# Prompt attention on one core: an extra full-array matmul into an unread bank at each of TensorE's two waits per unit

## The chip, the cores and the metric

The kernel runs on one core of a Trainium2 chip. The metric is the device time of one launch in microseconds (us). Three runs of the kernel before gave 5847.97, 5851.65 and 5852.48 us; their median is 5851.65 us.

## What is computed

The reference is one inference step of a trunk of two layers, for a prompt of 512 tokens and for 8 requests of 8 new tokens each. A layer projects the normalised rows, passes them through three mixers (pooling, dilated attention, a recurrent mixer), maps them back, and adds a block of retrieved experts. The change lies in the dilated attention of the prompt alone: 6 heads of width 64, where each query reads keys at three strides.

```python
def dilated_attn_prompt(q, k, v):
    scale = HEAD_DIM ** -0.5
    for window, dil in DILATED_GROUPS:            # (128, 1), (512, 4), (2048, 16)
        ...
        s = jnp.einsum('brnqhd,brnkhd->brnhqk', qr, kb, preferred_element_type=jnp.float32) * scale
        s = jnp.where(valid[None, None, :, None], s, NEG_INF)
        m = jnp.max(s, axis=-1, keepdims=True)
        p = jnp.exp(s - m)
        den = jnp.sum(p, axis=-1, keepdims=True)
        o = jnp.einsum('brnhqk,brnkhd->brnqhd', p / den, vb.astype(jnp.float32))
        ...
    return _combine_branches(outs, lses).astype(q.dtype)
```

The kernel joins the three branches into one softmax over all 512 keys: how often a query reads a key enters as the logarithm of that count, added to the scores (0 times is a large negative number).

## The kernel before

`program` (from L2199) loops over the two layers. In each, `attend_prompt` (L475) comes after `rotate` and before `attend_sample`; it is a stage of its own, with all engines starting it together and ending it together.

Its work is cut into 24 units, `units = [(qt, h) ...]`: four query tiles `qt` of 128 queries, and in each the six heads `h`. A unit of query tile `qt` reads `qt + 1` tiles of 128 keys, so units grow from one key tile (the first six) to four (the last six). For one unit:

- TensorE makes the scores, `scores(u)` at L505: the head's 64 rows of q against 128, 256, 384 or 512 keys, into one of three banks of `s_ps`. Only 64 of the array's 128 rows are in use.
- VectorE scales them and adds the logarithm of the counts (L559), and takes the maximum (L562). ScalarE takes the exponential with its sum (L535). VectorE inverts the sum (L577) and scales the row (L578), which gives semaphore `normed`.
- TensorE transposes the probabilities, 128 keys at a time, against the identity (L516) into `t_ps`; ScalarE copies them out (L545, semaphore `turned_in`).
- TensorE multiplies them with the values (L524): 64 columns of v, 128 rows, into `o_ps`. VectorE copies the result into `mixed` (L569).

All data are float32. In the trace a matmul of two float32 operands is two records, each with its own weight load; a transpose is one record.

TensorE's order is written out by hand. It first issues the scores of units 0, 1 and 2. Then, for each unit `u`: wait for `normed` of this unit; transposes of `u`; scores of `u + 3` (none for the last three units); wait for `turned_in` of this unit; values of `u`. VectorE and ScalarE run ahead of it: the probabilities and the transposed probabilities have two buffers each, the scores three banks.

`s_ps` takes three of the eight banks of the accumulation memory, `t_ps` and `o_ps` two each; one is free. Before unit 0 can be transposed, the counts `att_lc` have to arrive by DMA; they are issued at the stage's start. `m.ident` is the 128 by 128 identity, `m.proj` holds the projected rows (pooling input, q, k, v), 576 columns each.

Of the kernel before, what the change touches and what calls it, by code (L numbers as in the profile page):

```python
# [29 lines left out]
F32 = mybir.dt.float32  # L30
# [7 lines left out]
P = 128  # L38
# [55 lines left out]
def sbuf(nc, name, shape, dt):  # L94
    return nc.sbuf_tensor(f"{name}_{next(_serial)}", shape, dt)


def psum(nc, name, shape, dt):
    return nc.psum_tensor(f"{name}_{next(_serial)}", shape, dt)
# [15 lines left out]
@contextmanager  # L115
def stage(nc, *names):

    with ExitStack() as ctx:
        sems = namedtuple("Semaphores", names)(*(ctx.enter_context(nc.semaphore(f"{n}_{next(_serial)}")) for n in names))
        with nc.Block() as block:  # L120
            yield block, sems
        with nc.Block() as tidy:  # L122
            @tidy.sync
            def _(sp):
                for sem in sems:
                    sp.sem_clear(sem)
# [348 lines left out]
def attend_prompt(nc, m):  # L475


    units = [(qt, h) for qt in range(4) for h in range(HEADS)]
    with ExitStack() as ctx:
        sm = ctx.enter_context(sbuf(nc, "att_s", [P, 2, TP_], F32))  # L480
        pr = ctx.enter_context(sbuf(nc, "att_p", [P, 2, TP_], F32))
        pt = ctx.enter_context(sbuf(nc, "att_pt", [P, 2, 4, P], F32))
        st_ = ctx.enter_context(sbuf(nc, "att_stat", [P, 2, 4], F32))
        lc = ctx.enter_context(sbuf(nc, "att_lc", [P, 4, TP_], F32))
        s_ps = ctx.enter_context(psum(nc, "att_sps", [P, 3, TP_], F32))
        t_ps = ctx.enter_context(psum(nc, "att_tps", [P, 2, 4, P], F32))
        o_ps = ctx.enter_context(psum(nc, "att_ops", [P, 2, 512], F32))
        with stage(nc, "counts_in", "scored", "maxed", "expd", "normed", "turned", "turned_in", "valued",
                   "out_in", "dve_step", "stored") as (block, s):
            @block.sync  # L490
            def _(sp):
                sp.dma_start(lc[:], m.dram.count_prompt).then_inc(s.counts_in, 16)
                sp.dma_start(m.dram.out_k[m.l], m.proj[:, BK:BK + PAIRS, :]).then_inc(s.stored, 16)
                sp.dma_start(m.dram.out_v[m.l], m.proj[:, BV:BV + PAIRS, :]).then_inc(s.stored, 16)
                sp.wait_ge(s.stored, 32)

            @block.tensor
            def _(pe):
                def scores(u):
                    qt, h = units[u]  # L500
                    c, o = h // 2, 64 * (h % 2)
                    n = (qt + 1) * P
                    if u >= 3:
                        pe.wait_ge(s.maxed, u - 2)
                    nc.tensor.matmul(s_ps[:, u % 3, 0:n], m.proj[o:o + 64, BQ + c, qt * P:(qt + 1) * P],  # L505
                                     m.proj[o:o + 64, BK + c, 0:n], start=True, stop=True).then_inc(s.scored, 1)

                for u in range(3):
                    scores(u)
                for u, (qt, h) in enumerate(units):  # L510
                    c, o = h // 2, 64 * (h % 2)
                    pe.wait_ge(s.normed, u + 1)
                    if u >= 2:
                        pe.wait_ge(s.turned_in, u - 1)
                    for b in range(qt + 1):
                        ins = nc.tensor.transpose(t_ps[:, u % 2, b, :], pr[:, u % 2, b * P:(b + 1) * P], m.ident[:])  # L516
                    ins.then_inc(s.turned, 1)
                    if u + 3 < len(units):
                        scores(u + 3)
                    pe.wait_ge(s.turned_in, u + 1)  # L520
                    if u >= 2:
                        pe.wait_ge(s.out_in, u - 1)
                    for b in range(qt + 1):
                        ins = nc.tensor.matmul(o_ps[o:o + 64, u % 2, 0:P], m.v_tok[:, b, h * HD:(h + 1) * HD],  # L524
                                               pt[:, u % 2, b, :], start=(b == 0), stop=(b == qt))
                    ins.then_inc(s.valued, 1)

            @block.scalar
            def _(act):
                def exps(u):  # L530
                    n = (units[u][0] + 1) * P
                    act.wait_ge(s.maxed, u + 1)
                    if u >= 2:
                        act.wait_ge(s.turned, u - 1)
                    nc.scalar.activation(pr[:, u % 2, 0:n], sm[:, u % 2, 0:n], ACT.Exp, bias=st_[:, u % 2, 0:1],  # L535
                                         accum_out=st_[:, u % 2, 1:2]).then_inc(s.expd, 1)

                exps(0)
                for u, (qt, h) in enumerate(units):
                    if u + 1 < len(units):  # L540
                        exps(u + 1)
                    act.wait_ge(s.turned, u + 1)
                    if u >= 2:
                        act.wait_ge(s.valued, u - 1)
                    nc.scalar.activation(pt[:, u % 2, 0:qt + 1, :], t_ps[:, u % 2, 0:qt + 1, :],  # L545
                                         ACT.Copy).then_inc(s.turned_in, 1)

            @block.vector
            def _(dve):
                st = Steps(dve, s.dve_step)  # L550
                dve.wait_ge(s.counts_in, 16)

                def mask_max(u):
                    qt = units[u][0]
                    n = (qt + 1) * P
                    dve.wait_ge(s.scored, u + 1)
                    if u >= 2:
                        dve.wait_ge(s.expd, u - 1)
                    st.link(nc.vector.scalar_tensor_tensor(out=sm[:, u % 2, 0:n], in0=s_ps[:, u % 3, 0:n],  # L559
                                                           scalar=HD ** -0.5, in1=lc[:, qt, 0:n],  # L560
                                                           op0=ALU.mult, op1=ALU.add))
                    nc.vector.tensor_reduce(st_[:, u % 2, 0:1], sm[:, u % 2, 0:n], X, ALU.max,  # L562
                                            negate=True).then_inc(s.maxed, 1)

                def collect(u):
                    qt, h = units[u]
                    c, o = h // 2, 64 * (h % 2)
                    dve.wait_ge(s.valued, u + 1)
                    nc.vector.tensor_copy(m.mixed[o:o + 64, 2 + c, qt * P:(qt + 1) * P],  # L569
                                          o_ps[o:o + 64, u % 2, 0:P]).then_inc(s.out_in, 1)  # L570

                mask_max(0)
                mask_max(1)
                for u, (qt, h) in enumerate(units):
                    n = (qt + 1) * P
                    dve.wait_ge(s.expd, u + 1)
                    st.link(nc.vector.reciprocal(st_[:, u % 2, 2:3], st_[:, u % 2, 1:2]))  # L577
                    nc.vector.tensor_scalar(pr[:, u % 2, 0:n], pr[:, u % 2, 0:n], st_[:, u % 2, 2:3], None,  # L578
                                            ALU.mult).then_inc(s.normed, 1)
                    if u + 2 < len(units):  # L580
                        mask_max(u + 2)
                    if u >= 1:
                        collect(u - 1)
                collect(len(units) - 1)
# [1827 lines left out]
```

## Time and profile before

| | us |
|---|---|
| median of three runs | 5851.65 |
| the profiled execution, device time | 5854.53 |
| its span, from first to last instruction | 5852.7 |
| TensorE matmul busy | 5207.9 (89% of the span) |
| TensorE weight load busy | 4825.6 (82%) |
| VectorE busy | 3272.7 (56%) |
| ScalarE busy | 1733.5 (30%) |
| GpSimd busy | 353.5 (6%) |

The profile comes from one execution; positions are counted from its first instruction. Most of the span is the experts' block, where TensorE is busy over 90%. The stage that is changed stands at about 223 to 307 us in the first layer and 3140 to 3221 us in the second, so some 160 us of the whole.

The profile lists the clock that the chip granted TensorE in each stretch, as a share of 2.4 GHz: 1.00 is 2.4 GHz and 0.50 is 1.2 GHz, and there is no third level on this core. The mean over the span is 0.914. A group of matmuls is listed with its start, its extent and its count; a matmul's extent reaches past the start of the next one, since matmuls are pipelined, so what one of them costs is read from the distance between starts.

### The profile page before, as it was taken

To read this page: it belongs to the slowest core of one execution; us is meant where nothing else is said; L and a number is where in the kernel's file an instruction comes from. 1 tells how busy PE (TensorE), PEld (TensorE's weight loads), DVE (VectorE), ACT (ScalarE), POOL (GpSimd) and SP (SyncE) were. 2 spreads that over 40 slices of the span, in tenths; PEclk is the share of its full clock that TensorE was granted. 3 is DMA by queue.
4 is the path that set the end of the run, shared out by engine and by line. 5 is a ranking of instruction groups with operands and counts; after the bars stand their busy time and mean duration, and the time that the engine had idled before them with its cause. 6 is when DMAs were issued, how large, how long until landed. Compare 5 with 4: busy or idle time off the path is not lost. (4 is left out here: it accounts for less than half of the span.)

```text
span 5852.7 us, 96170 instructions
## 1 busy us (share of the span) xinstructions
PE 5207.9 (89%) x36954; PEld 4825.6 (82%) x36954; DVE 3272.7 (56%) x7049; ACT 1733.5 (30%) x2854; POOL 353.5 (6%) x192
## 2 busy tenths in 40 slices
PE   6887877888999999999978878678889999999998
PEld 6636747888999999999966367478889999999998
DVE  2436456777555555556724354577875555555567
ACT  2213213278222222222122132122872222222222
POOL 0010004400000000000000100045000000000000
PEclk9787768999999999999987877789999999999999
DMA  2150002256433323334321500121564332333253
GB/s 84 44 188 3 0 36 84 68 148 198 172 117 126 126 112 119 126 119 162 126 73 38 190 0 0 49 78 64 171 196 158 126 119 112 126 126 118 106 180 127
DMA packets 387666, 631.22 MB, mean 108 GB/s; under 512 B 25952, under 2 KB 324448, under 8 KB 345632
## 3 DMA queue, kind: packets, MB, share of 16 engines
q1 hardware_dynamic: 387488, 628.99, 30.8%
q8 instruction: 94, 1.54, 0.1%
q14 instruction: 84, 0.69, 0.0%
HBM read 526.51 MB, written 152.36 MB: 116 GB/s over the span
## 5 line engine op out<-in xcount | busy, mean ns | idle before, releaser
L235 PE MATMUL ex_op<-ex_ah,ex_vl 128*128 128x288 f32 x3584 | 1064.2, 297 | 7.4 <-DVE ex_acc L2081 6.4
L237 PE MATMUL ex_op<-ex_ah,ex_vh 128*128 128x288 f32 x3584 | 1059.5, 296 | 0.0
L236 PE MATMUL ex_op<-ex_al,ex_vh 128*128 128x288 f32 x3584 | 1058.7, 295 | 0.0
L2081 DVE TENSOR_TENSOR ex_acc<-ex_acc,ex_op 128x576 f32<-128x576 f32 x896 | 672.7, 754 | 551.4 <-PE ex_op L237 544.3
L235 PE MATMUL ex_hp<-x_hi,ex_ul 128*128 128x288 f32 x3072 | 907.0, 295 | 37.9 <-PEq L122 37.9
L237 PE MATMUL ex_hp<-x_hi,ex_uh 128*128 128x288 f32 x3072 | 907.7, 295 | 0.0
L236 PE MATMUL ex_hp<-x_lo,ex_uh 128*128 128x288 f32 x3072 | 906.8, 295 | 0.0
L235 PEld LDWEIGHTS ex_op<-ex_ah,ex_vl 128*128 128x128 f32 x3584 | 674.9, 188 | 14.9 <-DVE ex_acc L2081 14.9
L237 PEld LDWEIGHTS ex_op<-ex_ah,ex_vh 128*128 128x128 f32 x3584 | 675.0, 188 | 0.0
L236 PEld LDWEIGHTS ex_op<-ex_al,ex_vh 128*128 128x128 f32 x3584 | 674.9, 188 | 0.0
L235 PEld LDWEIGHTS ex_hp<-x_hi,ex_ul 128*128 128x128 f32 x3072 | 578.6, 188 | 38.3 <-issue 38.3
L2030 ACT ACTIVATE ex_vh<-ex_v 128x2048 fp32r<-128x2048 f32 x128 | 245.5, 1918 | 1141.9 <-PE ex_op L237 862.4
L236 PEld LDWEIGHTS ex_hp<-x_lo,ex_uh 128*128 128x128 f32 x3072 | 578.6, 188 | 0.0
L237 PEld LDWEIGHTS ex_hp<-x_hi,ex_uh 128*128 128x128 f32 x3072 | 578.5, 188 | 0.0
L2084 DVE TENSOR_TENSOR ex_a<-ex_a,ex_g 128x576 f32<-128x576 f32 x192 | 145.6, 758 | 634.2 <-ACT ex_a L2044 633.7
L2044 ACT ACTIVATE ex_a<-ex_hp 128x576 f32<-128x576 f32 x192 | 124.9, 651 | 799.1 <-PE ex_hp L237 799.1
L1789 PE MATMUL g_ps<-g_a,g_a 128*128 128x128 f32 x2304 | 314.1, 280 | 46.9 <-DVE g_a L1752 22.8
L1789 PEld LDWEIGHTS g_ps<-g_a,g_a 128*128 128x128 f32 x2304 | 289.8, 194 | 58.2 <-DVE g_a L1752 38.8
L2073 DVE TENSOR_TENSOR ex_vl<-ex_v,ex_vh 128x2048 fp32r<-128x2048 f32 x128 | 292.5, 2285 | 0.0
L235 PE MATMUL rt_qps<-x_hi,rt_wl 128*128 128x288 f32 x512 | 161.4, 315 | 100.3 <-ACT rt_q L1607 84.9
L235 PE MATMUL proj_ps<-x_hi,proj_w_lo 128*128 128x288 f32 x704 | 211.7, 301 | 41.3 <-DVE proj_w_lo L317 41.3
L1752 DVE TENSOR_SCALAR g_a<-iota,i1T,gT 128x128 f32<-128x128 f32 x864 | 248.3, 350 | 0.0
(366 smaller groups left out, 9939.6 us busy)
## 6 DMA issues: line engine op xcount, KB each, us to landing
ex_u<-in_peer_uT SPq DMA_DIRECT2D x128, 1024.0 KB, 7.6
ex_v<-in_peer_v SPq DMA_DIRECT2D x128, 1024.0 KB, 6.8
gate_matrix<-g_stage SPq DMA_DIRECT2D x18, 4096.0 KB, 15.9
ex_g<-gate_matrix SPq DMA_DIRECT2D x128, 576.0 KB, 5.0
dec_k<-in_cache_kT SPq DMA_DIRECT2D x16, 1536.0 KB, 7.1
dec_v<-in_cache_v SPq DMA_DIRECT2D x16, 1536.0 KB, 7.5
out_s_k<-in_cache_k_kept SPq DMA_DIRECT2D x128, 190.5 KB, 6.2
out_s_v<-in_cache_v_kept SPq DMA_DIRECT2D x128, 190.5 KB, 6.2
```

What stands on the lines that cost most here:

```text
L235: nc.tensor.matmul(out, w_lo, x_hi, start=first, stop=False)
L236: nc.tensor.matmul(out, w_hi, x_lo, start=False, stop=False)
L237: return nc.tensor.matmul(out, w_hi, x_hi, start=False, stop=last)
L1752: ins = nc.vector.tensor_scalar(a1[:, b % 4, n, :], m.iota[:], i1T[:, t], gT[:, t], ALU.is_equal, ALU.mult)
L1789: ins = nc.tensor.matmul(ps[:, q, n, :], a2[:, q, n, :], a1[:, q, n, :], start=True, stop=True)
L2030: nc.scalar.activation(v_hi[:, j], v_raw[:, j], ACT.Copy).then_inc(s.vh, 1)
L2044: nc.scalar.activation(a_raw[:, e, :].rearrange("p (a t) -> p a t", a=2), hp[:, e, :, 0:HALF], ACT.Gelu).then_inc(s.gelud, 1)
L2073: nc.vector.tensor_tensor(v_lo[:, j], v_raw[:, j], v_hi[:, j].bitcast(F32), ALU.subtract).then_inc(s.vl, 1)
L2081: nc.vector.tensor_tensor(a, a, o[:, :, 0:HALF], ALU.add).then_inc(s.added, 1)
L2084: nc.vector.tensor_tensor(a_raw[:, e, :].rearrange("p (u t) -> p u t", u=NU), h.rearrange("p (u t) -> p u t", u=NU), gb[:, j, :, e, :], AL ...
```

## The change

TensorE gets a bank of its own, `warm`, that nobody reads, and a helper `keep_busy` that issues one float32 matmul into it: the identity as weights (128 by 128), 256 columns of `m.proj` as the moving operand. The helper is called twice per unit: ahead of the wait for `normed`, and ahead of the wait for `turned_in`. Nothing else moves, and no wait is added or removed.

```diff
@@ -485,6 +485,7 @@
         o_ps = ctx.enter_context(psum(nc, "att_ops", [P, 2, 512], F32))
+        warm = ctx.enter_context(psum(nc, "att_warm", [P, 512], F32))
@@ -507,8 +508,13 @@
                 for u in range(3):
                     scores(u)
+                def keep_busy():
+
+                    nc.tensor.matmul(warm[:, 0:256], m.ident[:], m.proj[:, 0, 0:256], start=True, stop=True)
+
                 for u, (qt, h) in enumerate(units):
                     c, o = h // 2, 64 * (h % 2)
+                    keep_busy()
                     pe.wait_ge(s.normed, u + 1)
@@ -517,6 +523,7 @@
                     if u + 3 < len(units):
                         scores(u + 3)
+                    keep_busy()
                     pe.wait_ge(s.turned_in, u + 1)
```

Over two layers of 24 units that is 96 matmuls, 192 records of matmul and 192 weight loads.

## Rows read from the trace of the kernel before

**Rows 1.** Stretches: us, length, busy PE PEld DVE ACT POOL, clock.
```profile
225.50:296.80 71.30, 65.42 (x177) 33.95 (x177) 38.29 (x110) 19.88 (x64) 0.00 (x0) 0.50 0.10 38
296.80:306.30 9.50, 7.33 (x47) 5.11 (x46) 3.49 (x11) 3.79 (x8) 0.00 (x0) 0.98 0.00 0
3140.60:3208.70 68.10, 60.58 (x164) 31.19 (x163) 36.04 (x105) 19.19 (x62) 0.00 (x0) 0.50 0.12 42
3208.70:3220.70 12.00, 9.82 (x61) 6.49 (x60) 5.76 (x15) 5.08 (x11) 0.00 (x0) 1.00 0.00 0
285.86:290.81 4.95, 4.95 (x16) 2.78 (x15) 2.37 (x6) 1.30 (x3) 0.00 (x0) 0.50 0.02 3
```

**Rows 2.** What TensorE waited for, 231.3 to 296.8 us: total, times, longest.
```profile
PE att_tps L516 <- DVE att_p L578: 7.4, 1, 7.4
```

**Rows 3.** First transpose and last copy of the stage, layer one, layer two.
```profile
231.38 0.48 PE L516 MATMUL att_tps<-ident,att_p 128*128 128x128 f32 x1 [7.45 <-DVE att_p L578]
...
306.23 0.29 DVE L569 COPY mixed<-att_ops 64x128 f32<-64x128 f32 x1 [2.08 <-PE att_ops L524]
...
3148.20 0.48 PE L516 MATMUL att_tps<-ident,att_p 128*128 128x128 f32 x1 [7.52 <-DVE att_p L578]
...
3220.62 0.29 DVE L569 COPY mixed<-att_ops 64x128 f32<-64x128 f32 x1 [2.08 <-PE att_ops L524]
```

**Rows 4.** TensorE in order of time at 1.2 GHz, units of one key tile.
```profile
233.13 0.48 PE L516 MATMUL att_tps<-ident,att_p 128*128 128x128 f32 x1
...
234.87 0.48 PE L516 MATMUL att_tps<-ident,att_p 128*128 128x128 f32 x1
...
237.03 1.22 PE L505 MATMUL att_sps<-proj 64*128 64x256 f32 x2
238.18 0.69 PE L524 MATMUL att_ops<-att_pt,v_tok 128*64 128x128 f32 x2
```

**Rows 5.** The same, single records, in a unit of three key tiles.
```profile
260.95 0.42 PE L524 MATMUL att_ops<-att_pt,v_tok 128*64 128x128 f32 x1
...
261.30 0.48 PE L516 MATMUL att_tps<-ident,att_p 128*128 128x128 f32 x1
...
262.13 1.01 PE L505 MATMUL att_sps<-proj 64*128 64x384 f32 x1
...
262.93 0.84 PE L505 MATMUL att_sps<-proj 64*128 64x384 f32 x1
...
263.71 0.47 PE L524 MATMUL att_ops<-att_pt,v_tok 128*64 128x128 f32 x1
```

**Rows 6.** Single records of `rotate`, a full-array float32 matmul after a pause.
```profile
217.53 0.85 PE L354 MATMUL rope_ps<-proj,rope_swap 128*128 128x288 f32 x1 [0.18 <-DVE proj L375]
...
218.17 0.66 PE L354 MATMUL rope_ps<-proj,rope_swap 128*128 128x288 f32 x1
```

**Rows 7.** TensorE in order of time, where the clock rises, layer one.
```profile
290.81 1.12 PE L516 MATMUL att_tps<-ident,att_p 128*128 128x128 f32 x4
...
295.75 1.12 PE L516 MATMUL att_tps<-ident,att_p 128*128 128x128 f32 x4
296.80 1.29 PE L505 MATMUL att_sps<-proj 64*128 64x512 f32 x2
```

**Rows 8.** TensorE in order of time at 2.4 GHz, units of four key tiles, layer two.
```profile
3210.77 0.66 PE L516 MATMUL att_tps<-ident,att_p 128*128 128x128 f32 x4
3211.35 1.12 PE L505 MATMUL att_sps<-proj 64*128 64x512 f32 x2
3212.41 1.09 PE L524 MATMUL att_ops<-att_pt,v_tok 128*64 128x128 f32 x8
3213.43 0.66 PE L516 MATMUL att_tps<-ident,att_p 128*128 128x128 f32 x4
...
3215.79 0.66 PE L516 MATMUL att_tps<-ident,att_p 128*128 128x128 f32 x4
```

**Rows 9.** Stretches (columns as rows 1) with nothing on TensorE but transposes of L228.
```profile
884.30:887.60 3.30, 2.87 (x14) 2.49 (x13) 3.19 (x8) 0.11 (x1) 0.00 (x0) 0.50 0.00 0
888.00:891.00 3.00, 1.46 (x11) 0.86 (x9) 2.68 (x6) 2.04 (x4) 0.00 (x0) 1.00 0.00 0
```

## The prediction

> **What bounds the kernel now.** I read the clock first, then who waits, then the distances between starts. In both layers the prompt's attention runs at 1.2 GHz for all but its last 10 to 12 us: the granted clock is 0.50 over 71.3 us in the first layer and 68.1 us in the second [rows 1]. The list of waits for the first of these stretches has one entry, the 7.4 us before the first transpose, when the counts are still on their way by DMA [rows 2]. Behind it TensorE waits for nobody; in a unit of four key tiles it is listed busy for all of its 4.95 us while VectorE has 2.37 us of work [rows 1]. So at 1.2 GHz the two waits at which the change puts its matmuls are waits in the program and not in time. TensorE is the bound of this stage, and the stage is on the path of the whole: everything after it starts when it ends.
>
> The part that the change can move runs from the first transpose to the last copy: 306.23 - 231.38 = 74.85 us and 3220.62 - 3148.20 = 72.42 us, together 147.3 us [rows 3].
>
> **What a unit costs now.** The step between starts is what one thing adds. At 1.2 GHz a unit with one key tile takes 234.87 - 233.13 = 1.74 us [rows 4], one with four 295.75 - 290.81 = 4.94 us [rows 7]. So each key tile adds (4.94 - 1.74)/3 = 1.07 us. A record streams its columns twice at this clock: 128 columns are 0.213 us, and a key tile is one transpose, two records of scores, two of values: 5 x 0.213 = 1.07, as found. The 0.68 us left per unit (1.75 - 1.07) is not streaming. Single records show where it sits [rows 5]. From the last value record to the first transpose there are 0.35 us where 0.213 would do, so 0.14 us go where the shape in use changes (64 columns to 128 columns). From scores to values it is 0.78 for 0.64 us of streaming, again 0.14. Between the two records of one score matmul it is 0.80 for 0.64: 0.16 us more. The same 0.16 us stand between the two records of a full-array matmul after a pause: 0.64 us for 0.48 [rows 6]. The rest is a third change of shape (0.14) and 0.05 us in the transposes and in the values each.
>
> At 2.4 GHz a unit of four key tiles with scores takes 3213.43 - 3210.77 = 2.66 us, of which 20 x 0.107 = 2.13 stream and 0.53 do not; without scores, where it waits for ScalarE's copy, 3215.79 - 3213.43 = 2.36 [rows 8].
>
> **What the change adds.** Each call is two full-array records of 256 columns, 2 x 0.427 = 0.85 us at 1.2 GHz and 0.43 at 2.4.
> - The call ahead of `turned_in` stands between scores (64 rows) and values (64 columns), so there are two changes of shape instead of one, and its own second record is late. The nearest row is the pair of score records of the same 256 columns with the change behind it: 238.18 - 237.03 = 1.15 us [rows 4]. At 2.4 GHz the score pair of 512 columns takes 3212.41 - 3211.35 = 1.06 for 0.85 of streaming [rows 8], so 0.20 beside the streaming, and this call costs 0.43 + 0.20 = 0.63.
> - The call ahead of `normed` has the shape of the transposes that follow, so it takes over their change of shape instead of adding one: 0.85 + 0.16, less the 0.05 that the transposes lose no more, is 0.96 us; at 2.4 GHz 0.43 + 0.11 - 0.06 = 0.48.
>
> Together 2.11 us per unit at 1.2 GHz and 1.11 at 2.4. The bounds, since the trace has no such call between these neighbours: if the second records follow with no gap, 1.79 and 0.90. I take the upper pair, as [rows 6] is a full-array float32 matmul. Free are only the first call of each layer (it falls into the 7.4 us wait [rows 2]) and part of those in the last three units, where TensorE waits for ScalarE: there the second call fits under the wait and the first costs 0.48, so 2.36 becomes 2.84. The bank is the free one, no DMA and no other engine's instruction is added; VectorE's 2.37 us per unit at most stay below every new TensorE unit of that size.
>
> So a unit takes, with q key tiles of its own and k in the scores it issues: at 1.2 GHz 0.68 + 0.64q + 0.43k + 2.11, at 2.4 GHz 0.53 + 0.32q + 0.21k + 1.11. For three units each in turn (the scores run three units ahead) that is 3.86, 4.28, 4.92, 5.35, 5.99, 6.42, 7.06 us at 1.2 GHz and 2.17, 2.39, 2.71, 2.92, 3.24, 3.45, 3.77 at 2.4; the last three units come to about 8.1 us to the last copy. All at 2.4 GHz the part would take 3 x 20.65 + 8.1 = 70.1 us. A unit at 1.2 GHz costs more by 1.69, 1.89, 2.21, 2.43, 2.75, 2.97, 3.29.
>
> **When the clock rises.** This decides the size. The clock cannot be kept up from the stage before, since TensorE idles for the DMA and the stage starts at 0.50 as now; every number depends on how many units pass before it rises. Now it rises at 296.80, in the 21st unit [rows 7], and in the second layer at 3208.7, in the 20th [rows 1], so in units of four key tiles. Such a unit holds 2.56 us of work on 128 rows and 1.71 on 64 rows in 4.95 us. The six of three key tiles before them, at their smallest 1.92 and 1.28 in 3.88, did not raise it. With the change the 1st to 3rd unit hold 2.35 and 0.43 in 3.86 us, the 4th to 6th 2.35 and 0.85 in 4.28, the 7th to 9th 2.99 and 0.85 in 4.92. The last is the first that is like the unit in which the clock rose: more full-row work, less half-row work, the same time. The added gaps are why the small units do not get there: the calls bring 1.71 us of full-row work and 0.40 us of nothing. I take the rise after eight units, 35 us in. Then a layer takes 70.1 + 3 x 1.69 + 3 x 1.89 + 2 x 2.21 = 85.3 us, two take 170.5, and the change is 170.5 - 147.3 = +23 us. Against the profiled execution that is 5854.5 + 23 = 5877.5; the median of the runs lies 2.9 us below it, so I say 5875 us.
>
> **A rule weighed.** TensorE is listed busy without a wait for 65 us at clock 0.50 [rows 1]. The Trainium skill, TensorE: Matmul & The Clock Gate, Part 1, says that the throttled clock is the default and that sustained matmul activity releases it; by that the stage ought to be at full clock already, and the trace disagrees. It is a rule for the change all the same, and stands among the rivals. Of transposes: in 884.3 to 887.6 us nothing else ran on TensorE, 14 records, and the clock went from 0.50 to 1.00 behind them [rows 9], so I count them with the full-row work. Of transposes the Trainium skill says in TensorE: Matmul & The Clock Gate, Part 4, that they do not count as activity in the same way; this trace disagrees.
>
> **The rivals.**
> - *Early rise.* The full-array matmuls raise the clock within the first three units. A layer is then 70.1 + 1.7 to 5.1 us, two are 143.6 to 150.4: -4 to +3 us, 5848 to 5855, no difference. With a rise after five units it is 70.1 + 5.1 + 3.8 = 79.0, +10.7: still inside. For it: the calls bring 1.71 us of full-row work into units that had 0.64. Against it: the mix above. Chance 0.17. The rule of the Trainium skill above, TensorE: Matmul & The Clock Gate, Part 1, would give this case.
> - *Faster.* The early rise, and a second record that follows without a gap, and no added change of shape: then only 0.86 us per unit at 2.4 GHz, a layer of 70.1 - 21 x 0.25 = 64.9 and 1.7 for the first unit, two 133: -14 us, 5838. It decides only if the rise comes by the first or second unit (break-even with the bound below at -11.7). Against it stand [rows 5, 6]. Chance 0.05.
> - *Late rise.* The gaps keep the clock down until the units of three key tiles are well under way. After 12 units it is 70.1 + 10.7 + 6.6 + 7.3 = 94.7, +42; after 15 units 103, +59 us, 5911. For it: the 10th to 12th unit hold 2.99 and 1.28 in 5.35, no denser than the 7th. Chance 0.10 beyond +51.
> - *It does not do what it says.* The matmul is meant for a wait; if TensorE is never idle there, it fills nothing. This holds for all units at 1.2 GHz [rows 2], and is in the sum.
>
> **How the numbers follow.** The likeliest case, a rise between the end of the 6th and of the 13th unit (+14 to +51 us with the spread of the runs), has 0.65 and gives 5875. The rest is a sum just short of it (+11.7 to +14, 0.03), the early rise 0.17, faster 0.05, late 0.10. A measurement of this kernel can tell 0.2% from no change, 11.7 us. Slower by more: 0.65 + 0.03 + 0.10 = 0.78. Within: 0.17. Faster: 0.05. The forecast with the lower bound for the calls (8 units x 0.32 + 15 x 0.21, 5.7 us less per layer) is +12, and with a rise one unit sooner +7. The range has to reach further, into the early rise, until about 0.05 of that case, the faster one and the late one are all that is left out (0.20): from 5851, a rise within two units, to 5903, a rise after 13 units (+48) with the spread of the runs.
>
> **What would show it.** Right: the stage starts at clock 0.50, starts of transposes in the first units 3.9 us apart, two `att_warm` records 0.59 us apart, the rise near 265 and 3182 us, then 2.7 us per unit. Wrong: distances of 3.4 us or less (no gaps), a rise before 243 us, or one after 287 us, or the other engines' waits showing up in the small units at 2.4 GHz, since I have priced those with TensorE alone.

## The result and the profile after

| | before | after |
|---|---|---|
| median of 6 runs each | 5852.06 us | 5872.82 us |
| the profiled execution, device time | 5854.53 | 5865.93 |
| its span | 5852.7 | 5864.1 |
| mean granted clock | 0.914 | 0.921 |
| the stage, first transpose to last copy, layer one | 74.85 | 85.37 |
| the same, layer two | 72.42 | 82.91 |

The change makes the kernel slower: 1.0033 times the time before, with a 95% interval of 1.002 to 1.0045, so 12 to 26 us; the medians differ by 20.8 us. The clock is up for longer, and the time is longer all the same. The forecast was 5875.

The stretches that answer to [rows 1] (from, to, length, busy PE PEld DVE ACT POOL, granted clock):

```profile
225.30:266.20 40.90, 34.89 (x80) 17.91 (x80) 14.12 (x50) 6.88 (x28) 0.00 (x0) 0.50 0.18 66
266.20:316.70 50.50, 49.69 (x237) 29.64 (x236) 27.92 (x70) 16.80 (x44) 0.00 (x0) 1.00 0.00 1
3143.70:3181.30 37.60, 31.61 (x75) 16.23 (x76) 12.47 (x45) 7.14 (x26) 0.00 (x0) 0.50 0.22 75
3181.30:3234.70 53.40, 52.57 (x251) 31.29 (x249) 29.59 (x75) 17.67 (x47) 0.00 (x0) 1.00 0.00 1
```

The stage runs at 1.2 GHz for 41 and 38 us instead of 71 and 68, and at 2.4 GHz for 50 and 53 us instead of 10 and 12. TensorE is busy all through the second part too, 49.69 of 50.50 us. The waits of TensorE from 231.2 to 266 us, the answer to [rows 2], are again one entry; from 266.3 to the end there are three short ones, in the last three units:

```profile
PE att_tps L522 <- DVE att_p L585: 6.9, 1, 6.9
...
PE att_ops L531 <- ACT att_pt L552: 0.8, 3, 0.3
```

The ends of the stage that answer to [rows 3], the first transpose and the last copy (the first transpose of layer one is in the next fence):

```profile
316.68 0.29 DVE L576 COPY mixed<-att_ops 64x128 f32<-64x128 f32 x1 [2.56 <-PE att_ops L531]
...
3151.76 0.48 PE L522 MATMUL att_tps<-ident,att_p 128*128 128x128 f32 x1 [5.99 <-DVE att_p L585]
...
3234.67 0.29 DVE L576 COPY mixed<-att_ops 64x128 f32<-64x128 f32 x1 [2.56 <-PE att_ops L531]
```

TensorE in order of time, the first unit, then the starts of the 7th to the 9th with the rise, then units at 2.4 GHz and one of the last three; these answer to [rows 4, 7, 8]:

```profile
231.31 0.48 PE L522 MATMUL att_tps<-ident,att_p 128*128 128x128 f32 x1 [6.87 <-DVE att_p L585]
...
232.44 1.22 PE L513 MATMUL att_warm<-proj,ident 128*128 128x256 f32 x2
233.59 0.69 PE L531 MATMUL att_ops<-att_pt,v_tok 128*64 128x128 f32 x2
234.21 1.22 PE L513 MATMUL att_warm<-proj,ident 128*128 128x256 f32 x2
235.22 0.42 PE L522 MATMUL att_tps<-ident,att_p 128*128 128x128 f32 x1
...
239.08 0.42 PE L522 MATMUL att_tps<-ident,att_p 128*128 128x128 f32 x1
...
255.80 0.64 PE L522 MATMUL att_tps<-ident,att_p 128*128 128x128 f32 x2
...
260.73 0.63 PE L522 MATMUL att_tps<-ident,att_p 128*128 128x128 f32 x2
...
265.66 0.63 PE L522 MATMUL att_tps<-ident,att_p 128*128 128x128 f32 x2
266.22 0.72 PE L506 MATMUL att_sps<-proj 64*128 64x256 f32 x2
...
268.62 0.38 PE L522 MATMUL att_tps<-ident,att_p 128*128 128x128 f32 x2
...
271.52 0.38 PE L522 MATMUL att_tps<-ident,att_p 128*128 128x128 f32 x2
...
308.59 0.60 PE L522 MATMUL att_tps<-ident,att_p 128*128 128x128 f32 x4
...
309.88 1.09 PE L531 MATMUL att_ops<-att_pt,v_tok 128*64 128x128 f32 x8 [0.25 <-ACT att_pt L552]
...
311.43 0.60 PE L522 MATMUL att_tps<-ident,att_p 128*128 128x128 f32 x4
```

The call between scores and values costs 233.59 - 232.44 = 1.15 us, the one ahead of the transposes 235.22 - 234.21 = 1.01, and the transposes behind it are listed at 0.42 instead of 0.48, the 0.05 that they lose no more. Units are 3.86 us apart (239.08 - 235.22), the 7th and 8th 4.93 (260.73 - 255.80, 265.66 - 260.73), and the rise falls into the 9th unit, at 266.2; in layer two it came at 3181.3, as the 8th unit began.

### The profile page after: what moved, and what is told of

Read it like the earlier page. It is cut to its first block and busy times, and to the rows that moved or that the text cites. A ratio compares the mean times of both kernels' runs of the same rounds, so it can differ in the third digit from the quotient of the medians.

```text
span 5864.1 us, 96554 instructions
## 1 busy us (share of the span) xinstructions
PE 5226.0 (89%) x37146; PEld 4835.5 (82%) x37146; DVE 3273.8 (56%) x7049; ACT 1735.1 (30%) x2854; POOL 354.1 (6%) x192
```

## The experiments

After the result one theory stood against several rivals. The theory is the one of the prediction: a call costs its streaming plus the gaps of its place, at the clock of the moment, and the clock rises when the units hold enough work on full rows. The rivals were that the place of a call does not matter, that the rise is tied to time or to the count of units, that columns count on however many rows, and that the added matmuls are to blame whatever the clock. The edits below are against the changed kernel; in all of them what TensorE adds goes into the unread bank, and the outputs do not depend on it. Stage times are from the first transpose to the last copy in the profiled execution, with 147.3 us before for the two layers. The times of the kernel before that are given beside a run were measured along with it.

**One call per unit, ahead of `normed`.**

```diff
                     if u + 3 < len(units):
                         scores(u + 3)
-                    keep_busy()
                     pe.wait_ge(s.turned_in, u + 1)
```

> Only the call ahead of the wait for normed is left in each unit. Theory (a call costs its streaming plus the gaps of its place, and the clock rises where the mix of full-row work is dense enough): the call has the shape of the transposes behind it, so it costs 0.96 us per unit at 1.2 GHz and 0.48 at 2.4. A layer all at 2.4 GHz would take 56.6 us from the first transpose to the last copy; a unit at 1.2 GHz costs 1.2 us more in the first three, then 1.4, 1.7, 1.9, 2.2. The rise comes later than with both calls, between the 9th and the 15th unit, so 70 to 79 us per layer against 73.6 before: -7 to +12 us in all, most likely about +2 (ratio 1.000). Rival (every call costs the same 0.85 us of streaming wherever it stands, and half the calls cost half of the change): half of +21, so +10 us, and the same as with the second call only.

Measured: 5869.59 us against 5854.77, ratio 1.0027 (1.0018 to 1.0037). The stage took 77.73 and 82.09 us, +12.5 in all. The stretches at 1.2 GHz:

```profile
224.30:278.90 54.60, 48.31 (x124) 26.18 (x121) 23.16 (x75) 12.46 (x44) 0.00 (x0) 0.50 0.15 52
...
3146.10:3207.60 61.50, 56.34 (x143) 31.16 (x144) 27.04 (x85) 13.84 (x49) 0.00 (x0) 0.50 0.11 40
```

The rise came in the 14th unit of layer one, at 278.9, and just as the 16th of layer two began, at 3207.6 (its transposes start at 3207.3), at the late edge of what was expected and one unit past it; with the rise where it was, the sum gives 56.6 + 3.5 + 4.2 + 5.1 + 5.8 + 2.4 = 77.6 us for the first layer and 77.73 were measured. So the unit prices hold, and my guess for the rise (+2 us, so near the end of the 12th unit) was too early by more than one unit in layer one and by three in layer two. Half of the calls is more than half of the cost, 12.5 of 21.0 us in the stage: with fewer matmuls the clock stayed down for longer.

**One call per unit, ahead of `turned_in`.**

```diff
                     c, o = h // 2, 64 * (h % 2)
-                    keep_busy()
                     pe.wait_ge(s.normed, u + 1)
```

> Only the call ahead of the wait for turned_in is left in each unit. Theory: it stands between scores on 64 rows and values on 64 columns, so it adds a change of shape; it costs 1.15 us per unit at 1.2 GHz and 0.63 at 2.4, and leaves the units less dense than the first call does, so the clock rises later, between the 13th and the 19th unit. A layer all at 2.4 GHz would take 58.4 us; 80 to 88 us per layer against 73.6 before: +13 to +29 us, most likely +20, and so 10 us or more above the kernel with the first call only. Rival (the place does not matter): the same as with the first call only, +10 us.

Measured: 5875.38 us, ratio 1.0037 (1.0024 to 1.0049), +20.6 us on the medians. The stage took 92.73 and 80.53 us, +26.0. The stretches at 1.2 GHz:

```profile
226.10:308.00 81.90, 76.19 (x184) 37.46 (x184) 33.84 (x100) 17.28 (x58) 0.00 (x0) 0.50 0.09 33
...
3158.10:3216.10 58.00, 50.47 (x124) 24.74 (x124) 23.10 (x75) 12.82 (x44) 0.00 (x0) 0.50 0.15 49
```

The first layer reached the 19th unit before the rise, the second the 14th. With half of the change's matmuls the cost is all of the change's, and 5.8 us more than with the other call (medians; the two intervals overlap). That is the sign that the theory gave, at a smaller size than the 10 us it named, and by itself no proof. The distances between starts settle whether the place matters. Here are the second and third unit of layer one, first with the call ahead of `normed`, then with the one ahead of `turned_in`:

```profile
234.80 0.42 PE L522 MATMUL att_tps<-ident,att_p 128*128 128x128 f32 x1
...
237.51 0.42 PE L522 MATMUL att_tps<-ident,att_p 128*128 128x128 f32 x1
```

```profile
234.71 0.48 PE L521 MATMUL att_tps<-ident,att_p 128*128 128x128 f32 x1
...
237.61 0.48 PE L521 MATMUL att_tps<-ident,att_p 128*128 128x128 f32 x1
```

The unit takes 2.71 us with the one and 2.90 with the other, against 1.74 before: 0.97 and 1.16 us for the same columns, where 0.96 and 1.15 had been summed.

**512 columns in each call.**

```diff
-                    nc.tensor.matmul(warm[:, 0:256], m.ident[:], m.proj[:, 0, 0:256], start=True, stop=True)
+                    nc.tensor.matmul(warm[:, 0:512], m.ident[:], m.proj[:, 0, 0:512], start=True, stop=True)
```

> Both calls stream 512 columns instead of 256. Theory: 1.71 us more per unit at 1.2 GHz, 0.86 at 2.4, the gaps as they are. The first unit then holds 4.1 us of full-row work in 5.6 us and the clock rises within the first three units of each layer, not after the eighth. A layer takes about 90 us and 2.5 us for each unit before the rise: 92 to 98 us, so +37 to +48 us in all (ratio 1.006 to 1.008). Rival (the rise is tied to the time or to the count of units and not to the mix): it comes again some 30 to 35 us in or after eight units, and the layer takes 105 us or more, +63 us.

Measured: 5880.01 us, ratio 1.0047 (1.0031 to 1.0064). The stage took 91.42 and 91.24 us, +35.4, and the clock rose as the second unit began, 5.8 and 5.4 us after the first transpose:

```profile
224.20:237.80 13.60, 8.06 (x14) 2.70 (x12) 3.57 (x15) 2.39 (x8) 0.00 (x0) 0.50 0.63 207
237.80:323.40 85.60, 85.58 (x308) 39.03 (x306) 38.44 (x104) 22.04 (x65) 0.00 (x0) 1.00 0.00 1
```

This excludes a rise tied to time or to the count of units. It also shows that an early rise alone is no gain: 85.6 us at 2.4 GHz, TensorE busy for all of them. The stage cost within 2 us of the lower edge that was expected; the whole kernel cost only 25 us, since the rest of it was 12 us shorter in the profiled execution. I come back to this below.

**Calls on 64 rows.**

```diff
-                    nc.tensor.matmul(warm[:, 0:256], m.ident[:], m.proj[:, 0, 0:256], start=True, stop=True)
+                    nc.tensor.matmul(warm[:, 0:256], m.ident[0:64, :], m.proj[0:64, 0, 0:256],
+                                     start=True, stop=True)
```

> Both calls use 64 of the 128 rows of the array (the upper half of the identity and of the moving operand), with the same 256 columns. Theory (work on 64 rows counts half for the clock): the calls bring the same streaming but half of the work, the clock stays at 1.2 GHz until the units of four key tiles or to the end of the stage, and the change costs +70 to +110 us (ratio 1.012 to 1.019). For odd heads the second call may run beside the scores, which sit on the other 64 rows; that only lowers the cost of a unit, by up to 0.8 us. Rival (what counts is the time in which columns stream, on however many rows): the rise comes as with the full rows, within about nine units, and the change costs +10 to +22 us.

Measured: 5907.13 us, ratio 1.0086 (1.0058 to 1.0114); single executions from 5874 to 5933. The profiled one, 5933, is at 1.2 GHz for the whole of both stages, 117.5 us each:

```profile
224.30:350.40 126.10, 119.28 (x324) 63.38 (x324) 41.86 (x120) 24.82 (x73) 0.00 (x0) 0.50 0.07 23
3180.20:3303.70 123.50, 117.46 (x316) 62.29 (x316) 41.80 (x119) 23.70 (x72) 0.00 (x0) 0.50 0.06 22
```

TensorE is busy for 119 of 126 us, the rest is the wait for the DMA, and the clock never rises in the stage. The columns and the places in the program are those of the changed kernel; the rows are halved, and the calls can run beside scores on the other half of the rows, so the first units take 3.3 to 3.75 us instead of 3.86 and TensorE is no less occupied. So for the clock a matmul on 64 rows was worth less than one on 128, and being busy without a wait was not enough to raise it. The overlap, in every second unit, is a second difference, and no run here parts it from the rows. The other executions lie lower, by up to 59 us. Their mean granted clock over the whole kernel goes with the time: 0.906 and 0.907 at 5933 and 5932 us, 0.911 or 0.912 around 5900 to 5908, 0.917 at 5874. So in some of them the clock was probably up for a part of the stage; where, was not recorded. Five of the six still lie above every execution of the changed kernel.

**A burst in the wait for the DMA, no call in any unit.**

```diff
+                for _ in range(14):
+                    keep_busy()
                 for u, (qt, h) in enumerate(units):
                     c, o = h // 2, 64 * (h % 2)
-                    keep_busy()
                     pe.wait_ge(s.normed, u + 1)
...
-                    keep_busy()
                     pe.wait_ge(s.turned_in, u + 1)
```

> No call per unit. Instead 14 calls stand in a row after the first three scores, in the 7 us in which TensorE waits for the counts' DMA: 14 x 0.43 = 6.0 us at 2.4 GHz, so they are free and the clock is at 2.4 GHz when unit 0 is transposed. Theory (holding the clock needs work too): the units of one key tile hold only 0.43 us of work in the 1.5 us that VectorE needs for one, the clock falls again within the first six units, and the rest goes as in the kernel before, with the rise in the last units: 70 to 74 us per layer, -7 to 0 us in all. Rival (once up it stays up while TensorE is in use): 49 us per layer, -50 us in all.

Measured: 5849.45 us, ratio 0.999 (0.9973 to 1.0007), single executions from 5821 to 5874. The stage took 74.5 us in both layers. But the clock was not lost in the small units, it was lost at the very first of them:

```profile
223.92 6.31 PE L513 MATMUL att_warm<-proj,ident 128*128 128x256 f32 x28
232.17 0.33 PE L523 MATMUL att_tps<-ident,att_p 128*128 128x128 f32 x1 [1.95 <-DVE att_p L585]
...
232.50:297.40 64.90, 64.90 (x177) 33.65 (x176) 36.46 (x103) 18.88 (x60) 0.00 (x0) 0.50 0.01 3
```

The burst ended 1.95 us before the first transpose (1.87 in layer two), and within 0.4 us behind that start the clock was at 0.50 and stayed there for 65 us. So this run did not test what I had meant it to.

**The burst, and the call ahead of `normed` in units 1 to 11.**

```diff
                     c, o = h // 2, 64 * (h % 2)
-                    keep_busy()
+                    if 1 <= u < 12:
+                        keep_busy()
                     pe.wait_ge(s.normed, u + 1)
```

(with the burst of 14 as above, and no call ahead of `turned_in`)

> The same 14 calls in the wait for the DMA, and the call ahead of normed in units 1 to 11 only. Theory: the clock is at 2.4 GHz from the first transpose on and is held; the first twelve units take 1.54, 1.75, 2.07 and 2.28 us (three each, the call at 0.48 us included), the next nine 2.2, 2.35 and 2.66, the last three 2.36 less the end: 51 us per layer against 73.6, -45 us in all (ratio 0.992). Rival (the clock falls in spite of the calls): 70 us or more per layer, no gain beyond -7 us. Second rival (at 2.4 GHz another engine bounds the small units, which I have priced with TensorE alone): 55 to 60 us per layer, -27 to -37 us.

Measured: 5846.59 us, ratio 0.9991 (0.9969 to 1.0013), and twelve executions on three levels: four from 5812 to 5818, six from 5844 to 5851, two at 5884. The profiled one is of the first kind, with 50.78 us in both layers, as summed (51):

```profile
223.66 7.59 PE L513 MATMUL att_warm<-proj,ident 128*128 128x256 f32 x28
231.67 0.33 PE L525 MATMUL att_tps<-ident,att_p 128*128 128x128 f32 x1 [0.42 <-DVE att_p L587]
...
226.30:282.50 56.20, 53.63 (x267) 32.79 (x265) 40.93 (x120) 23.68 (x72) 0.00 (x0) 1.00 0.11 40
```

Here part of the burst ran at 1.2 GHz, so it took 7.59 us and ended 0.4 us before the transpose. The levels lie some 34 us apart; the reading that a layer either keeps the clock or loses it at its start fits, and the next run shows one of each.

**The same with the call in units 1 to 5 only.**

```diff
-                    if 1 <= u < 12:
+                    if 1 <= u < 6:
```

> As the one before, but the call only in units 1 to 5. Theory: if the units of two key tiles hold the clock by themselves (0.85 us of full-row work in the 1.85 us that VectorE needs), a layer takes 49.5 us, -48 us in all, 3 us better than with twelve. If they don't, the clock falls in the second quarter and the layer takes 62 us or more, -22 us at best; their mix lies just above what the clock was lost with elsewhere, so I give the two an even chance.

Measured: 5827.94 us, ratio 0.9947 (0.9929 to 0.9966). Layer one took 48.07 us at 2.4 GHz throughout, layer two 77.05:

```profile
3109.35 6.31 PE L513 MATMUL att_warm<-proj,ident 128*128 128x256 f32 x28
3117.30 0.33 PE L525 MATMUL att_tps<-ident,att_p 128*128 128x128 f32 x1 [1.64 <-DVE att_p L587]
...
3117.90:3182.70 64.80, 64.80 (x172) 33.75 (x171) 33.92 (x96) 17.78 (x58) 0.00 (x0) 0.50 0.01 4
```

Again the burst ended early, by 1.64 us, and the clock fell at the start of the units, in the first of them and so before the units of two key tiles were reached. Those did not lose it: in layer one, where the clock was up, it held through the units of two key tiles with no call in them. The first transpose of layer one came 0.51 us behind its burst.

**The change with the burst ahead of it.** Both calls in all units, as in the changed kernel, and the burst of 14.

```diff
+                for _ in range(14):
+                    keep_busy()
                 for u, (qt, h) in enumerate(units):
```

> The changed kernel with both calls in all units, and the 14 calls in the wait for the DMA ahead of them. It measures what the first eight units at 1.2 GHz cost, and the price of the calls at 2.4 GHz. Theory: all units run at 2.4 GHz, 70.1 us per layer (2.17, 2.39, 2.71, 2.92, 3.24, 3.45, 3.77 us for three units each, 8.1 us for the last three) against 85.4 and 82.9 with the change: 28 us less than the changed kernel, and -7 us against before. Rival (the added matmuls make the stage slower by themselves, the clock hardly matters): no more than 5 us less than the changed kernel.

Measured: 5840.68 us, ratio to before 0.998 (0.9971 to 0.999), and 32 us less than the changed kernel (medians). The stage took 69.67 us in both layers, where 70.1 had been summed:

```profile
223.00:301.00 78.00, 75.69 (x348) 46.00 (x346) 41.94 (x120) 24.39 (x73) 0.00 (x0) 1.00 0.11 37
3132.80:3208.20 75.40, 74.22 (x341) 44.77 (x339) 41.96 (x120) 23.68 (x72) 0.00 (x0) 1.00 0.08 30
```

So the first seven to eight units at 1.2 GHz cost the change 15.7 us in layer one (85.37 - 69.67) and 13.2 in layer two. Without them it would be a small gain, of 11 us. In layer one the burst ended 1.49 us before the first transpose, and the clock was kept all the same.

**A burst of 18, calls in units 1 to 5.** The burst is made long enough to last until the first transpose.

```diff
-                for _ in range(14):
+                for _ in range(18):
```

> The burst has 18 calls instead of 14, so at 2.4 GHz it ends within a few tenths of a us of the first transpose, where the burst of 14 left TensorE idle for 1.6 us and the clock was lost (second layer of the run with calls in units 1 to 5). Theory (that pause, not the mix of the units, lost the clock): both layers take 48 us as the first layer of that run did, and perhaps 0.5 us of the burst stands past the end of the wait: -51 us in all, 5801 (ratio 0.991), in nearly all executions. Rival (units of one and two key tiles lose the clock by chance of where they fall): the times scatter as before, in steps of some 30 us, between 5800 and 5865.

Measured: 5808.72 us against 5851.47, ratio 0.9925 (0.9912 to 0.9939); five executions from 5805 to 5811. The stage took 48.07 and 48.01 us:

```profile
224.90 8.04 PE L513 MATMUL att_warm<-proj,ident 128*128 128x256 f32 x36
233.37 0.33 PE L525 MATMUL att_tps<-ident,att_p 128*128 128x128 f32 x1 [0.44 <-DVE att_p L587]
...
224.00:281.40 57.40, 54.58 (x274) 33.81 (x274) 40.52 (x119) 25.54 (x73) 0.00 (x0) 1.00 0.15 50
3117.80:3172.20 54.40, 52.24 (x262) 31.93 (x261) 40.63 (x120) 24.25 (x72) 0.00 (x0) 1.00 0.11 40
...
3114.82 9.50 PE L513 MATMUL att_warm<-proj,ident 128*128 128x256 f32 x36
3124.16 0.27 PE L525 MATMUL att_tps<-ident,att_p 128*128 128x128 f32 x1
```

The scatter is gone. In layer one the bracket behind the first transpose says 0.44 us, and the burst does not delay it: it still waits for VectorE. In layer two the burst ran at 1.2 GHz for its first 3 us, took 9.50 us instead of 8.04, and did delay it: there is no bracket, VectorE had scaled the first row by 3123.0, and the transpose came at 3124.16, 1.15 us later. This is faster than both kernels, by 43 us than the one before and by some 64 than the changed one. The two stages are 51.2 us shorter than before, as expected, but the profiled execution only 45.8. Of the 5.4 us between, 2.8 stand ahead of the first transpose: from the first scores to it there are 9.08 and 10.12 us, where before had 8.13 and 8.23. The rest is not accounted for.

**A burst of 18, calls in units 1 to 11.** The edit is the two above together.

> The same burst of 18, with the call in units 1 to 11. Theory: 50.8 us in both layers, -45 us in all, 5807, in nearly all executions, so some 5 us above the one with calls in units 1 to 5. Rival (the calls in units 6 to 11 are needed to hold the clock): this one is steady and the other scatters, and this is the faster.

Measured: 5811.73 us, ratio 0.9934 (0.9919 to 0.9949), 50.73 and 50.72 us in the two layers; four executions from 5810 to 5816. As steady as the one before and 3 us slower, with an interval that overlaps: the six calls more cost 2.7 us per layer and hold nothing that was not held. The burst ran into 1.2 GHz in both layers and held the first transpose up by 1.1 and 1.5 us.

**A burst of 18, no call in any unit.**

```diff
-                    if 1 <= u < 6:
-                        keep_busy()
```

> The burst of 18 and no call in any unit. Theory (a unit of one key tile without a call, 0.43 us of full-row work in 1.5 us, does not hold the clock): the clock starts at 2.4 GHz and is lost in the first six units, then rises late as before: 70 to 74 us per layer, -7 to 0 us. Rival (only the pause mattered, and the units hold the clock by themselves): 46 to 49 us per layer, -50 us or better, and the calls in the units are waste.

Measured: 5815.39 us, ratio 0.9929 (0.9908 to 0.995), four executions at 5800, 5802, 5828 and 5830. The profiled one, 5830, has a layer of each kind:

```profile
223.00:238.60 15.60, 14.60 (x69) 10.39 (x67) 7.62 (x31) 5.64 (x20) 0.00 (x0) 1.00 0.53 182
238.60:289.80 51.20, 51.20 (x137) 26.53 (x138) 27.98 (x75) 15.04 (x44) 0.00 (x0) 0.50 0.00 1
...
3138.00:3192.90 54.90, 52.05 (x264) 32.10 (x262) 40.33 (x119) 25.66 (x73) 0.00 (x0) 1.00 0.16 53
```

In layer one the clock was lost at 238.6, in the 6th unit, and the layer took 69.27 us; layer two held it and took 46.60. From the first transpose to that fall TensorE was listed busy for 6.12 of 6.58 us, so it was not a long pause that lost the clock there. The units were the same in both layers. So both theories were half right: units of one key tile without a call can lose the clock, but need not, and what decides it is open. The two fast executions lie below all five with calls in units 1 to 5. The five calls buy steadiness, for 1.4 us per layer, as far as five executions against four can tell.

## Why the prediction was right, point by point

**The bound.** TensorE waits for nobody at the two places. Shown by the waits of the changed kernel, with one entry ahead of the rise. The calls fill no idle time but in the last three units.

**The price of a call.** Summed 2.11 us per unit at 1.2 GHz and 1.11 at 2.4. Units of 3.86, 4.28 and 4.92 us were forecast, 3.86, 4.29 (247.23 - 242.94 in the same view) and 4.93 measured; at 2.4 GHz 2.92 and, for the last three, 2.84 were forecast, 271.52 - 268.62 = 2.90 and 311.43 - 308.59 = 2.84 measured. The bound without gaps (1.79 and 0.90) is out. The rows that priced the gaps [rows 4 to 6] carried this, though none of them showed the new operation: a pair of score records of the same 256 columns cost 1.15 us, and so did the call.

**The rise.** Put after eight units at 35 us; it came 34.9 us after the first transpose in layer one, in the 9th unit, and 29.5 us in layer two, in the 8th. The comparison of the mix of full-row and half-row work with that of the unit in which the clock had risen was right here, and the run on 64 rows shows that rows matter. As a rule for other mixes it was looser: with one call it put the rise more than one unit early in one layer and three in the other. The two layers of one execution rose one unit apart with both calls, two with the first alone and five with the second alone, so the comparison gives a region and no point, and that the 9th unit was hit was in part luck.

**The sum.** 85.3 us per layer were forecast, 85.37 and 82.91 measured, +21.0 instead of +23 for the stage. The whole of the profiled execution grew by 11.4 us only: from the last copy of layer one to the first transpose of layer two it took 3151.76 - 316.68 = 2835.1 us where before took 2842.0, and from the last copy of layer two to the end 2.7 us less. The medians of six runs differ by 20.8, so I take this for the scatter of single executions (before alone ranges over 10.8 us); that is not shown. The term that was too large is the second layer's, by 2.4 us, since its clock rose a unit sooner. The run with 512 columns does not fit as well: its stage grew by 35.4 and its median by 25.2, with four executions within 7 us. Where those 10 us lie is open; the profile has them in pieces of 2 to 4.5 us in stages that the edit does not touch.

**The rivals.** The early rise is what the run with 512 columns and the one with the burst ahead show. With the calls of the change it is worth -11 us in the medians, where I had said -4 to +3 with one to three units at 1.2 GHz first. The last three units and the whole at 2.4 GHz were summed right (70.1 for 69.67), so 2 x 69.67 - 147.3 = -8 us is the stage's share, and 3 us of the -11 are not accounted for. The rule of the Trainium skill, TensorE: Matmul & The Clock Gate, Part 1, that sustained matmul activity releases the full clock, is not borne out as it stands: in the run with calls on 64 rows TensorE was busy for 117.4 of the 117.5 us from the first transpose to the last copy, on a mix of 64 and 128 rows, at 0.50. The rival on the faster side did not come, but its idea, the clock up from the first unit, is the one that pays once it is bought in the wait for the DMA instead of in the units.

**A premise that was wrong.** The prediction said that the clock cannot be kept up from the stage before, since the stage starts at 0.50. In the kernel before, the first three scores still run at 2.4 GHz, and the clock falls only at 225.5, in the wait for the DMA:

```profile
223.00:225.00 2.00, 0.68 (x6) 0.52 (x6) 0.00 (x0) 1.28 (x1) 0.00 (x0) 1.00 0.42 49
```

For the change this made no difference, as its first call is over long before the wait is. But the bursts could do what the premise ruled out: in both layers of the burst of 14 alone they ran at 2.4 GHz from their first call, so there they kept the clock that was up and did not raise it. In others, as in layer one of the run with calls in units 1 to 11, it had fallen just before they began and they raised it again.

## What to carry to other kernels

Before filling a wait with work, look whether it is a wait in time: an engine that is never idle there pays for each filler in full, with the gaps at each change of shape. If a stage starts at the low clock behind a DMA wait, put the filler into that wait, and let it last until the first real instruction; then add only what holds the clock. It is not quite free: a burst of 18 held the first transpose up by 1.1 to 1.5 us in three of six layers, and from the first scores to VectorE's first work on them there were 7.2 us on average in the 14 layers with a burst (6.6 to 7.6) against 6.6 in the 12 without (6.3 to 7.0), for a reason that these runs do not show. And price the filler by the nearest pair of records of the same size and neighbours, since the gaps between shapes were a fifth of its cost.

## What the runs showed of the hardware

- How long TensorE paused between the burst and the first transpose went with the clock that the small units then had. With 1.64, 1.87 and 1.95 us, and units without a call or with one, the clock was lost at the start (both layers of the burst of 14 alone, and the second of the run with calls in units 1 to 5), and all three of these layers then ran at 1.2 GHz for 65 us. With 0.33 to 0.56 us it was up as the units began, in the five layers whose bracket shows such a pause; in three of them the burst had also begun at 1.2 GHz and so lasted longer. One layer had 1.49 us and kept it; its units held both calls of the change. One of the five, of the run with no call in any unit, lost the clock 6.6 us later, with TensorE listed busy for 6.12 of them. So the pause is not all of it, and these runs do not part it from the work ahead of it and behind it, or from something else that differs between layers.
- The stage held the clock with less work than had failed to raise it: units of two key tiles without any call ran on at 2.4 GHz (run with calls in units 1 to 5, layer one), while in the kernel before, at 1.2 GHz, six units of three key tiles in a row did not raise it.
- Two matmuls on different halves of the rows overlap. In the kernel with calls on 64 rows, the call in a unit whose scores use the other half starts 0.01 us behind them:

```profile
233.27 0.58 PE L506 MATMUL att_sps<-proj 64*128 64x128 f32 x1
233.28 0.79 PE L512 MATMUL att_warm<-proj,ident 64*128 64x256 f32 x1
```
